# Strassen's scheme for the FFN up-projection, iterations 1 to 10: seven block products for eight, with the block sums on GpSimd

## The reference, cut to what matters

```python
def conv_ffn(h, w_in, conv_w, conv_b, w_out):
    u = h @ w_in
    up = jnp.pad(u, ((0, 0), (1, 1), (0, 0)))
    uc = up[:, :-2] * conv_w[0] + up[:, 1:-1] * conv_w[1] + up[:, 2:] * conv_w[2] + conv_b
    a, b = jnp.split(uc, 2, axis=-1)
    return (jax.nn.silu(a) * b) @ w_out
```

## Time and profile before

| | |
|---|---|
| median of three runs | 3112.48 us |
| the profiled execution: span | 3114.7 us |
| the same execution's mean granted TensorE clock | 0.995 of 2.4 GHz |
| VectorE (DVE) busy | 67% of the span |
| ScalarE (ACT) busy | 35% |
| HBM traffic | 93 GB/s over the span |

### The profile page before, as it was taken

One profiled execution on the slowest core, in us unless ns is written; L12 is line 12 of the kernel. 1 busy time (PEld: TensorE's weight loads), 2 busy tenths in 40 slices (PEclk: granted clock), 3 DMA queues, 4 the chain that ended last, 5 costly groups with the idle time before them and its releaser, 6 DMA issues.

```text
span 3114.7 us, 55088 instructions
## 1 busy us (share of the span) xinstructions
PE 3029.6 (97%) x21528; PEld 2782.9 (89%) x21528; DVE 2078.6 (67%) x4009; ACT 1081.5 (35%) x2252; POOL 404.7 (13%) x392
## 2 busy tenths in 40 slices
PE   8999999999999999999999999999999889999999
PEld 6899999886699999998876699999998669999999
DVE  7766666778757666668647576666667875766665
ACT  3332222346633222224335442232233663322221
POOL 3000000133310000003247310000012331000000
PEclk9999999999999999999999999999999999999999
DMA  8533323110023332331200223233321002222221
GB/s 339 210 134 121 108 107 135 62 58 1 28 96 136 125 130 92 125 108 53 76 31 8 96 97 127 93 130 121 114 97 58 1 1 95 75 75 81 67 67 48
DMA packets 47201, 290.18 MB, mean 93 GB/s; under 512 B 4945, under 2 KB 11345, under 8 KB 13265
## 3 DMA queue, kind: packets, MB, share of 16 engines
q1 hardware_dynamic: 47058, 288.21, 25.5%
HBM read 283.98 MB, written 4.21 MB: 93 GB/s over the span
## 4 chain that ended last, share of the span: by engine, by line
PE 89%; DVE 5%; ACT 2%; DMA 2%; issue 1%; POOL 0%; SPq 0%; POOLq 0%; DVEq 0%; ACTq 0%
PE psA L2087 38%; PE psB L2087 24%; PE psA L2196 4%; PE psA L2197 3%; PE psA L2202 3%; PE psA L2104 2%; PE psB L760 2%; PE psA L837 2%; PE psA L2283 1%; DMA w_stage<-weights_dram 1%; PE psB L742 1%; DVE top L1676 1%; PE psB L895 1%; PE psA L728 1%; PE psA L2288 1%
## 5 line engine op out<-in xcount | busy, mean ns | idle before, releaser
L2087 PE MATMUL psA<-h_hi,w_hi 128*128 128x320 f32 (+1 forms) x2736 | 625.0, 310 | 2.6 <-ACT u_raw L2475 1.7
L2087 PE MATMUL psA<-h_lo,w_hi 128*128 128x320 f32 (+1 forms) x2720 | 620.5, 309 | 0.0
L2087 PE MATMUL psA<-h_hi,w_lo 128*128 128x320 f32 x2704 | 616.1, 309 | 0.0
L2662 DVE SCALAR_TENSOR_TENSOR xT<-psB,mod,xT 128x128 f32<-128x128 f32 x750 | 377.5, 546 | 206.2 <-PE psB L2087 206.2
L2087 PEld LDWEIGHTS psA<-h_hi,w_hi 128*128 128x128 f32 x2736 | 455.9, 188 | 4.2 <-ACT u_raw L2475 2.5
L2087 PEld LDWEIGHTS psA<-h_lo,w_hi 128*128 128x128 f32 x2720 | 455.2, 188 | 0.0
L2087 PEld LDWEIGHTS psA<-h_hi,w_lo 128*128 128x128 f32 x2704 | 452.1, 188 | 0.0
L2726 DVE TENSOR_SCALAR conv<-u_raw,vec_sb 128x642 f32<-128x642 f32 x176 | 108.3, 615 | 441.3 <-ACT u_raw L2475 441.3
L2539 DVE TENSOR_TENSOR w_lo<-w_stage,w_hi 128x512 fp32r<-128x512 f32 x496 | 353.4, 756 | 33.4 <-ACT w_hi L2370 33.2
L2087 PE MATMUL psB<-g_hi,wo_hi 128*128 128x320 f32 x1280 | 296.3, 312 | 0.1
L2087 PE MATMUL psB<-g_hi,wo_lo 128*128 128x320 f32 x1280 | 294.9, 312 | 0.0
(11 more groups left out here) (272 smaller groups left out, 4953.0 us busy)
## 6 DMA issues: line engine op xcount, KB each, us to landing
w_stage<-weights_dram SPq DMA_DIRECT2D x124, 1024.0 KB, 5.1
m_stage<-w_mod_dram SPq DMA_DIRECT2D x96, 1024.0 KB, 8.4
wo_stage<-w_out_dram SPq DMA_DIRECT2D x44, 1024.0 KB, 4.7
yT_dram<-xT SPq DMA_DIRECT2D x8, 322.0 KB, 2.2
xT<-xT_dram SPq DMA_DIRECT2D x1, 1544.0 KB, 10.0
xT<-xT_dram SPq DMA_DIRECT2D x1, 1032.0 KB, 6.5
w_stage<-weights_dram SPq DMA_DIRECT2D x2, 512.0 KB, 17.9
rope_raw<-rope_dram SPq DMA_DIRECT2D x3, 256.0 KB, 2.7
```

The source lines that it names most:

```text
L2087: ins = pe.matmul(o, wp, xp[:, a:b], start=first and n == 0, stop=last and n == 2)
L2662: ins = dve.scalar_tensor_tensor(out=xT[:, d, c:c + w], in0=tokens(ps, slot)[i], scalar=gate[:, d, i:i + 1], in1=xT[:, d, c:c + w], op0=AL ...
```

## The change

For each pair `p` of iterations 1 to 10, the 2x2 blocks are: weights by tile (a, b) and by input half (`LOW`, `HIGH`: 4 blocks of 128 each), tokens by half (320 each) and by input half. Strassen's scheme needs seven products of 4 blocks each, 12 matmuls per product, in place of 96 matmuls for the two tiles. Products 0, 1 and 6 read weight blocks as loaded, or activations as they are; the others need sums. Iteration 0 stays as it was.

- Activations: four sums of 128x4x320 are made once per layer by GpSimd from a new float32 copy `h_f32` (written by ScalarE in `norm_act`, two more activations for each of 8 blocks), and split into `t_hi`, `t_lo`.
- Weights: GpSimd makes four sums of 128x512 for every pair (`w_sums` three, `w_last_sum` one). ScalarE and VectorE split seven units per pair (`split_product`, `product_lo`), 14 an iteration in place of 8. Unit `q` of pair `p` may be split once product `q` of the pair before it is done.
- Results: the products accumulate in one bank of psA each (q 0, 2, 4, 6 in bank 0 or 3, q 1 in bank 1, q 3 and 5 in bank 2), and partial sums are copied out between them: ScalarE after products 0, 2, 3, 4 and 6, VectorE adds after 1 and 5 (`add_first`, `add_second`), GpSimd adds the last half (`last_half`, 128x320). TensorE waits for a copy before the next product that accumulates in that bank.
- The first of the three convolution instructions moves from VectorE to ScalarE (`conv_begin`, an activation with scale and bias); `gated` becomes one instruction of 128x642 written in place; `g_hi` and `g_lo` become two instructions each.
- The order: the first pair's products, `out_pass` of the iteration before, the second pair's products. In iteration 10 both pairs run ahead of both passes. Modulation matmuls stand at both ends of `out_pass`, with loads of 1 MB into one buffer.

```diff
+                def w_sums(it, p):
...
+                    pool.wait_ge(s_w[p], it * 16 + 16 * (cf + 1))
...
+                        pool.wait_ge(s_slo, nth(l, it, p, PRODUCTS, 4 - PRODUCTS))
+                    a11, _, a21, a22 = (w_stage[:, 4 * p + i, :] for i in range(4))
+                    s1, s2 = w_part(it, p, 3), w_part(it, p, 2)
+                    pool.tensor_tensor(s1, a21, a22, ALU.add).then_inc(s_ss, 1)
+                    pool.wait_ge(s_ss, nth(l, it, p, 4, 1))
+                    pool.tensor_tensor(s2, s1, a11, ALU.subtract).then_inc(s_ss, 1)
+                    pool.tensor_tensor(a21, a11, a21, ALU.subtract).then_inc(s_ss, 1)
...
+                def w_last_sum(it, p):
+
+                    pool.wait_ge(s_slo, nth(l, it, p, PRODUCTS, 1))
...
+                def last_half(it, p):
+
+                    pool.wait_ge(s_ev, nth(l, it, p, 5, 4))
...
+                def sums(it):
+                    w_last_sum(it, 1)
+                    last_half(it, 0)
+                    w_sums(it + 1, 0)
+                    w_last_sum(it + 1, 0)
+                    last_half(it, 1)
+                    w_sums(it + 1, 1)
...
+                    bank = {1: 1, 3: 2, 5: 2}.get(q, 3 * p)
+                    for k in range(4):
+                        c = slice(k * P, (k + 1) * P)
+                        for n, (w, x) in enumerate(((w_hi, X_HI), (w_hi, X_LO), (w_lo, X_HI))):
+                            ins = pe.matmul(psA[:, bank, 0:HALF], w[:, q, c], x[q][:, k, :],
...
+                def to_first_half(it):
...
+                    conv_first(it - 1, 3)
+                    first_part(it, 0)
+                    silu(it - 1, 1)
...
+                    split_product(it, 0, 6)
+                    split_product(it, 1, 0)
+                    split_product(it, 1, 1)
+                    ghi(it - 1, 1)
+                    second_part(it, 0)
...
+                    conv_first(it, 0)
+                    fifth_part(it, 0)
+                    conv_first(it, 1)
```

More of the change, by code:

```diff
@@ L75 @@
 N_CHUNKS = FFN_CHUNK[-1] + ITERS
+PLAIN = [sum(MIX_CHUNKS[:l]) + l for l in range(DEPTH)]
+PRODUCTS = 7
 QKV_ORDER = {1: (2, 0, 1), 2: range(6), 3: (2, 0, 1)}
@@ L2081, in _ @@
+                sums(1)
+                with pool.Fori(2, ITERS - 1) as it:
+                    sums(it)
+                w_last_sum(ITERS - 1, 1)
+                last_half(ITERS - 1, 0)
+                last_half(ITERS - 1, 1)
         @block.tensor
@@ L2841, in _ @@
-                ffn_last(ITERS - 1)
+                it = ITERS - 1
+                to_first_half(it)
+                gate(it, 0)
+                product_lo(it, 1, 6)
+                add_first(it, 1)
+                add_second(it, 1)
+                convolve(it, 2, conv[1])
+                convolve(it, 3, conv_last)
+                out_add(it - 1, 0)
+                gate(it, 1, conv[1], conv_last, conv[1])
+                out_add(it - 1, 1)
+                glo(it, 0, conv[0], g_hi_last, g_lo_last)
@@ new lines, in _ @@
+                out_add(it - 1, 2)
+                glo(it, 1, conv[1], g_hi_last, g_lo_last)
+                if more:
+                    mod_copy_ffn(l, it, 0, mod_taken(0))
+                for d in range(3, KT):
+                    out_add(it - 1, d)
+                    if d < 7 and more:
+                        next_lo(d - 3)
+                    if d in (5, 7):
+                        half = d // 7
+                        c = slice(half * UNIT, (half + 1) * UNIT)
+                        dve.wait_ge(s_wohi, it * 2 + (2 * ITERS * l + half + 1))
+                        dve.tensor_tensor(wo_lo[:, :, c], wo_stage[:, :, c], wo_hi[:, :, c].bitcast(F32),
+                                          ALU.subtract).then_inc(s_wolo, 1)
@@ L2846, in _chunk @@
+                for d in range(KT):
+                    out_add(it, d)
+                    if d == 0 and more:
+                        mod_copy_ffn(l, it, 1, mod_taken(3))
+                    if d < 4 and more:
+                        next_lo(4 + d)
+                    if d == 4 and more:
+                        mod_bias(l + 1, it, mod_parts(psA), mod_pass(l, it) + 1)
 def _chunk(w):
```

855 lines of the change are left out of this document (560 added, 295 removed).

## The result

The changed kernel takes 3259.24 us (median of four runs, 3258.53 to 3262.69), the kernel before in the same session 3112.54 (3110.02 to 3116.06). The ratio is 1.0470, with a 95% interval of 1.0455 to 1.0484: slower by 4.7%, where 5% was forecast. The profiled execution took 3259.57 us, its span is 3257.8 us and its mean granted clock 0.970, against 0.995 before.

The account below looks back on a forecast made before the run. TensorE, busy for 97% of the span, was taken as the bound. Matmuls -140.8, steady iterations +194, starts +112 and ends -12 gave +153 on 3114.7: 3268, stated as 3270 us, 5% slower, range 3050 to 3340.

Parts of the forecast that it names:

- matmuls: FFN loop on TensorE: 24 fewer an iteration, 960 in 40 iterations at 146.7 ns each, -140.8 us.
- steady iterations: FFN loop, 8 per layer: TensorE waits 5.8 us an iteration, 6.9 in layer 3, together +194 us.
- starts: Start of each layer's FFN, iteration 1 included: waits mostly at product 2, 28 us a layer, +112 us.
- ends: Last passes of each layer: wait for g_hi_last, g_lo_last goes, wait behind w_lo is spread; -3 us a layer, -12.
- turns: VectorE instructions with two SBUF operands and GpSimd's SBUF-reading sums run one at a time, each waiting for the other.
- Product 4: First pair's products: ScalarE's copy of that bank stands behind g_hi and ends late; TensorE waits 1.7 us an iteration.
- Tile 2: In out_pass: first out_add comes late behind held-up convolutions; TensorE waits 4.1 us, 5.2 in layer 3.
- the walk: One steady iteration timed from its first product: GpSimd's sum at 13.9, convolutions to 21.9, first out_add ending at 22.9 us.
- Rival 1: Loop and starts: GpSimd's sums and VectorE's two-SBUF-operand instructions exclude each other; 3270 us, range 3190 to 3335; chance 0.55.
- Rival 3: At L3061, L3064 and w_sums: convolutions don't wait for GpSimd, so layer 0 to 2 loop waits are 0; 3030 us; chance 0.2.
- Rival 2: Loop: TensorE's waits move GpSimd's sums beside VectorE's PSUM work, hiding half of 306 us; 3115 to 3190; chance 0.18.
- Rival 4: Between products: ScalarE's PSUM copies late everywhere, 5 per pair by 0.3 us, +120 us, 3390 us; chance 0.07.

Follow-up runs that it names:

- last kernel: Changed kernel with activation sums moved to VectorE and the order on VectorE, ScalarE and GpSimd rearranged, same products: 3017.88 us, ratio 0.9683 to the kernel before.
- e1_write_only: Changed kernel with GpSimd's four weight sums per pair replaced by tiny powers and zero fills that hardly read SBUF (results wrong): 3046.09 us, ratio 0.9785.
- e10_fourth_add: Changed kernel, two out_add moved between convolution instructions, product 2's copy ahead of g_hi, GpSimd's next three weight sums waiting for the fourth out_add: 3103.79 us, ratio 0.9965.

## Why the prediction was right

The span of the profiled execution is 143.1 us longer than before, where +153 was summed. Cut at the same two places in each layer (the start of tile 2 in iteration 1's pass and in iteration 9's), with the matmuls that were taken away counted by themselves, it is made of this:

| term | predicted, us | measured, us |
|---|---|---|
| matmuls | -140.8 | -140.8 (count times 146.7 ns) |
| steady iterations | +194 | +195 |
| starts | +112 | +90 |
| ends, and all else | -12 | -2 |

Slower by the mechanism that was named, turns at the places that were named: that much was right. That the time is within 11 us of 3270 is in part luck. The starts were put 22 us too high, the ends 10 us too low, and the steady term came out by two errors that cancel, as follows.

**Matmuls, -140.8.** The last kernel's iterations show it to within 0.2 us; the 147 ns distance stayed wherever the clock did.

**Steady iterations, +194.** The forecast was 47.2 and 45.8 us. Seven of layer 2, from 2009.20 to 2337.86, average 46.95, and six of layer 3, from 2804.41 to 3082.61, average 46.37 (the row above is one of them). The places were right, the make-up was not. Product 4: 0.93 us of wait where 1.7 was predicted. Tile 2: 3.15 in layer 2 (3.30 less 0.15) where 4.1 was, and in layer 3 a gap of 4.48, so 4.3, where 5.2 was. All three were put 0.8 to 1.0 us too high. Over the 32 iterations the waits are 24 x 4.08 + 8 x 5.26 = 140 us, and not 194. In the iteration of the rows above product 3 ends at 2183.07, so that its first product began four times 1.76 us earlier, at 2176.03. Counted from there, GpSimd's first sum starts at 12.7 us (predicted 13.9), `w_lo` ends at 14.7 (15.8), the convolutions at 20.2 (21.9) and the first `out_add` at 21.2 (22.9): the walk is the same one, with the load earlier. What made up the other 55 us was a term that was not in the sum, the clock (below). That the two cancel to 1 us is luck.

**Starts, 28 us a layer.** They took 22.6 (90 over the four). Product 0's wait was 1.0 us, not 3.6; product 2's 13.3, as summed (13.4); product 6's 1.6; the first tile 2's 3.2 (predicted 2.5 for products 4 and 6 each, and 5). That is 19 us, to which the clock adds 2.7 (from 1932.1 to 1945.8 TensorE is busy for 5.43 us at half speed), and the writes of `h_f32` some 2 by the prediction, not measured apart: 24 us, one too many. The walk in turns was nearly right in length: from GpSimd's first sum (1906.93) to the end of the second `t_lo` (1939.94) it is 33.0 us, where 34.1 was summed. But it began 13.9 us after the first matmul and not 17.3, so that the `t_lo` came at 46.9 and not at 51.4. Product 2's wait of 13.3 us agrees only because product 0 took 1.0 us of the delay and not 3.6. The prediction named `t_lo` as what is late; it is, and `part_y`, which it did not name, comes 0.4 us after it.

**Ends, -12.** Next to nothing came off: the ends, without their matmuls, are 0.4 us shorter in each of layers 0 to 2 and 2.7 longer in layer 3, and everything outside the four FFNs is 3 us shorter. The prediction read the earlier trace rows wrongly. The chain of work leaves TensorE from 2299.22 to 2302.85, but TensorE did not wait there: its matmuls go on 147 ns apart until 2302.45, and the one gap is 0.45 us. At the second place the gap is 1.79 us, of which 1.6 are a wait; it goes, and product 4 of iteration 10 waits 0.8 us instead (gap 0.90).

**The costs.** A 128x512 sum was priced at 1.27 us and takes 1.30; 128x320 at 0.86 and takes 0.78; 128x1280 at 2.89, and the pair of 6.02 us beside one turn fits it. The convolution's start on ScalarE, 740 ns by the SiLU's row, takes 927; no wait of TensorE is put down to it. VectorE's own work was put at about 33 us an iteration; in the last kernel it is busy for 35.8, with some turns in it.

**The rivals.** Rival 1, turns as summed, held in mechanism. (Its upper end is 3330 by its own terms, 3270 + 40 + 20, not 3335.) Rival 3, convolutions that pass freely, fell by the rows of 1.85 and 1.68 us and by e1_write_only, whose 3046 us is near the 3030 given to this side: the price of a kernel without waits in the loop was about right. Rival 2, waits that move the sums to where they cost nothing, did not happen by itself; it had to be written into the order (e10_fourth_add). Rival 4, late copies, is one copy late, in one pair of two. Its removal gained nothing, for tile 2 took it up.

**The clock.** It was missing. The three waits account for 202 us; less 141 for the matmuls, that leaves 82 of the 143. Summed over all matmul starts in stretches granted half clock, the time above the normal distance is 66 us, against 10 before (distances of over 0.6 us, which are waits, left out). So 56 of the 82 us are the clock's. Most of the other 26 are waits too: the profile's idle time is 0.16 us shorter than the gap at each of the 78 waits (12 us), and products 0 and 6 wait 2.6 us at each start (10 us).

## What to carry to other kernels

When work is given to GpSimd, count it against VectorE as well wherever VectorE's next instructions read two operands from SBUF: in the rows above each such instruction lasted until 0.5 to 0.7 us after GpSimd's. Then ask whether TensorE waits for one of them, for only that reaches the span. Place the work beside instructions that read PSUM, and make GpSimd wait for that place if need be. A wait of TensorE that is taken away ahead of a later, independently set one is only handed on: look for the last such wait first, and walk the combined order again, since two moves that are good alone can cancel. A scheme that saves TensorE's time (here 4.5%) pays only as far as nothing else makes TensorE pause, and here pauses of 3 us cost more than they lasted.
